# A hybrid HGRN2 and pooling block: whole fp32 operands built by accumulating transfers, and the first token tile taken ahead of the meta rows

## What is computed

```python
z = jnp.concatenate([meta, x], axis=1)                     # 16 + 1024 rows
h = rms_norm(z, norm_w[l])
p = (h @ w_in[l] + b_in[l]).astype(f32)                    # 1040 x 1024 by 1024 x 8192
q, fz, iv, g_hg, u, g_pool, m_hg, m_pool = jnp.split(p, split_at, axis=-1)
...
y_hg = (o * jax.nn.silu(g_hg)) @ w_down_hg[l]
y_pool = (mixed * pool_scale[l] * jax.nn.silu(g_pool)) @ w_down_pool[l]
merged = jax.nn.sigmoid(m_hg) * y_hg + jax.nn.sigmoid(m_pool) * y_pool
z = z + merged @ w_out[l]
...
return rms_norm(z, final_norm_w)[:, N_META:]
```

## Time and profile before

| what | value |
|---|---|
| median of 3 runs | 1035.59 us (1034.6 to 1035.83) |
| the profiled execution's own time | 1035.04 us |
| its span in the profile | 1033.3 us |
| PE busy | 1011.4 us, 98% of the span |
| DVE busy | 815.1 us, 79% |
| ACT busy | 512.2 us, 50% |
| POOL busy | 99.8 us, 10% |

### The profile page before, as it was taken

One profiled execution on the slowest core, in us unless ns is written; L12 is line 12 of the kernel. 1 busy time (PEld: TensorE's weight loads), 2 busy tenths in 40 slices (PEclk: granted clock), 3 DMA queues, 4 the chain that ended last, 5 costly groups with the idle time before them and its releaser, 6 DMA issues.

```text
span 1033.3 us, 18578 instructions
## 1 busy us (share of the span) xinstructions
PE 1011.4 (98%) x7204; PEld 827.7 (80%) x7204; DVE 815.1 (79%) x1343; ACT 512.2 (50%) x860; POOL 99.8 (10%) x162
## 2 busy tenths in 40 slices
PE   7999999999999999999999999999999999999996
PEld 7767888888878888878888888888887888788885
DVE  7989787868787878777676778876678879988975
ACT  7764636363636353544453534344447436435664
POOL 6200000101010101010101010102110010000130
PEclk9999999999999999999999999999999999999999
DMA  7221111202020202022213121227883384558374
GB/s 279 52 82 63 42 62 31 74 21 83 22 83 22 83 22 78 27 72 83 82 42 112 42 95 59 92 82 267 305 289 103 118 324 149 214 185 325 79 166 124
DMA packets 46855, 117.18 MB, mean 113 GB/s; under 512 B 4880, under 2 KB 13072, under 8 KB 46768
## 3 DMA queue, kind: packets, MB, share of 16 engines
q1 hardware_dynamic: 23680, 70.33, 20.5%
q0 software_dynamic: 8976, 26.26, 8.0%
q10 hardware_dynamic: 14112, 19.41, 5.5%
HBM read 86.62 MB, written 29.36 MB: 112 GB/s over the span
## 4 chain that ended last, share of the span: by engine, by line
PE 89%; DVE 8%; issue 2%; ACT 1%; DMA 1%; POOL 0%; DVEq 0%; SPq 0%; ACTq 0%
PE acc L1622 74%; PE levels L1677 2%; PE miscs L1711 1%; PE miscs L1710 1%; PE miscs L1699 1%; DVE r_lo L2489 1%; PE acc L1564 1%; PE miscs L1504 1%; PE levels L1504 1%; DVE w_lo L1900 1%; PE levels L1622 1%; PE levels L1683 1%; PE miscs L1717 1%; PE miscs L1690 1%; PE miscs L1652 1%
## 5 line engine op out<-in xcount | busy, mean ns | idle before, releaser
L1622 PE MATMUL acc<-r_hi,w_hi 128*128 128x512 f32 x1200 | 331.0, 397 | 3.5 <-ACT second L994 1.1
L1622 PE MATMUL acc<-r_lo,w_hi 128*128 128x512 f32 x1200 | 328.4, 392 | 0.5 <-DVE r_lo L2489 0.4
L1622 PE MATMUL acc<-r_hi,w_lo 128*128 128x512 f32 x1200 | 322.0, 390 | 0.5 <-DVE w_lo L1900 0.5
L1622 PEld LDWEIGHTS acc<-r_lo,w_hi 128*128 128x128 f32 x1200 | 223.0, 188 | 53.5 <-issue 4.9
L1622 PEld LDWEIGHTS acc<-r_hi,w_lo 128*128 128x128 f32 x1200 | 225.1, 188 | 49.1 <-DVE w_lo L1900 1.0
L1622 PEld LDWEIGHTS acc<-r_hi,w_hi 128*128 128x128 f32 x1200 | 218.6, 188 | 50.2 <-DVE zq L1994 2.3
L904 ACT ACTIVATE w_hi<-sum 128x512 fp32r<-128x512 f32 x164 | 102.9, 628 | 166.9 <-DVE sum L1933 84.7
L1900 DVE TENSOR_TENSOR w_lo<-sum,w_hi 128x512 fp32r<-128x512 f32 x164 | 112.0, 687 | 51.2 <-ACT w_hi L904 50.5
L1900 DVE TENSOR_TENSOR w_lo<-raws,w_hi 128x512 fp32r<-128x512 f32 x120 | 82.2, 687 | 48.6 <-ACT w_hi L904 48.6
L904 ACT ACTIVATE w_hi<-raws 128x512 fp32r<-128x512 f32 x120 | 74.6, 623 | 27.3 <-PE acc L1622 25.4
L994 ACT ACTIVATE second<-acc,bias 128x512 f32<-128x512 f32 x31 | 21.2, 685 | 59.9 <-PE acc L1622 59.8
(11 more groups left out here) (312 smaller groups left out, 1307.5 us busy)
## 6 DMA issues: line engine op xcount, KB each, us to landing
raws<-in_wstream SPq DMA_DIRECT2D x80, 512.0 KB, 3.6
xin<-in_x SPq DMA_DIRECT2D x8, 512.0 KB, 6.3
a_spill<-gt POOLq DMA_DIRECT2D x16, 256.0 KB, 3.5
c_spill<-pg POOLq DMA_DIRECT2D x16, 256.0 KB, 2.7
comb<-in_wstream ACTq DMA_DIRECT2D x8, 512.0 KB, 6.5
comb_spill<-comb ACTq DMA_DIRECT2D x8, 512.0 KB, 4.1
smh_spill<-zq POOLq DMA_DIRECT2D x16, 256.0 KB, 4.4
stage<-a_spill ACTq DMA_DIRECT2D x4, 1024.0 KB, 10.2
```

Source lines behind the costliest of these rows:

```text
L1622: ins = pe.matmul(bank[:, :], weights, moving, start=n == 0 and i in (0, 1, y_first), stop=n == 3 * KH - 1, skip_group_check=True)
```

## The change

- `nw` is loaded by SP instead of ACT. SP's order becomes x tile 1, nw, meta, tiles 2 to 4, raw weights 0 and 1, then tiles 5 to 7, raw 2, tile 8.
- Tile 1 goes through all engines ahead of the meta tile (`turn` swaps the two).
- Each of tiles 1, 2, 3, 4, 6, 8 gets banks of its own turn (`h_banks` is a table by tile).
- The fp32 B11 is no longer copied by DVE and the fp32 B21 no longer by ACT. SP copies the finished high part to a whole buffer within SBUF (`begin_whole`), and POOL issues a transfer that adds the low part to it (`make_whole`), 1 MB each, B11 first, B21 second.
- ACT writes -B12 into V7's slot and B22 into a buffer of its own, and POOL's `make_v7` adds B22 to -B12 by an accumulating transfer. `make_v4` does the same with V6 onto B21; the sign goes into ACT's scale and DVE's `v4_low`.
- The second half of the lb chain on DVE (four small operations) moves from ahead of tile 3 to behind `low(16)`.
- `early_sum`, `low(2)`, `low(4)` and `b21_low` change places on DVE; `meta_product(0)` moves between products (0,0) and (0,1); transposes 5 to 8 move later by one or two half products; `keep_warm` has 26 matmuls instead of 38.

```diff
-WARM_UP = (16, 4, 4, 4, 4)
+WARM_UP = ((1, 16), (0, 1), (2, 2), (3, 3), (4, 2))
...
         v6_whole = b11_whole = at("b11_whole", [P, KH, HALF], F32, R_AT + R_V4 * 16384)
+        b21_whole = at("b21_whole", [P, KH, HALF], F32, R_AT + R_V4 * 16384 + 8192)
+        b22_whole = at("b22_whole", [P, KH, HALF], F32, R_AT + R_V7 * 16384)
...
+            def begin_whole(n):
+                if n:
+                    sp.wait_ge(S["whole_begun"], 16)
+                    sp.wait_ge(S["h_copied"], 4)
+                    dst, src = b21_whole, r_hi[R_B21]
+                else:
+                    sp.wait_ge(S["h_hi"], 4)
+                    dst, src = b11_whole, r_hi[R_B11]
+                sp.dma_start(dst[:, :, :], src[:, :, :].bitcast(F32)).then_inc(S["whole_begun"], 16)
...
+            load_x(1)
+            sp.dma_start(nw[:, :], norm_w[0:1, :].to_broadcast([P, D])).then_inc(S["norm_row_loaded"], 16)
             sp.dma_start(xin[0][0:META, :], meta[:, :]).then_inc(x_loaded[0], 16)
-            load_x(1)
             load_x(2)
...
             begin_third(0)
+            begin_whole(0)
+            begin_whole(1)
             begin_third(1)
...
+            def make_whole(n):
+                pool.wait_ge(S["whole_begun"], 16 * n + 16)
+                if n:
+                    pool.wait_ge(S["whole_made"], 16)
+                    pool.wait_ge(S["h_lo"], 4)
+                    dst, src = b21_whole, r_lo[R_B21]
+                else:
+                    pool.wait_ge(S["b11_lo"], 4)
+                    dst, src = b11_whole, r_lo[R_B11]
+                pool.dma_start(dst[:, :, :], src[:, :, :].bitcast(F32), accum_op=ALU.add).then_inc(S["whole_made"], 16)
+
+            def make_v7():
+                pool.wait_ge(S["v5_made"], 4)
+                pool.wait_ge(S["h_copied"], CHUNKS)
+                pool.dma_start(r_lo_f[R_V7][:, :, :], b22_whole[:, :, :], accum_op=ALU.add).then_inc(S["v7_made"], 16)
+
+            def make_v4():
+                pool.wait_ge(S["v6_made"], 2)
+                pool.wait_ge(S["whole_made"], 32)
+                pool.dma_start(b21_whole[:, :, :], v6_whole[:, :, :], accum_op=ALU.add).then_inc(S["v4_made"], 16)
...
-                act.activation(b12_whole[:, :, c], lower, ACT.Copy)
-                act.activation(r_lo_f[R_V7][:, :, c], upper, ACT.Copy).then_inc(S["h_copied"], 1)
+                act.activation(r_lo_f[R_V7][:, :, c], lower, ACT.Copy, scale=-1.0)
+                act.activation(b22_whole[:, :, c], upper, ACT.Copy).then_inc(S["h_copied"], 1)
...
-            def b11_copy(i):
-                lower, _ = banks_of(i)
-                dve.tensor_copy(b11_whole[:, :, (i - 1) * P:i * P], lower)
...
             def v5_sum(i):
                 dve.wait_ge(S["h_copied"], i)
-                dve.tensor_tensor(r_lo_f[R_V6][:, :, piece(i)], b11_whole[:, :, piece(i)], b12_whole[:, :, piece(i)],
-                                  ALU.subtract).then_inc(S["v5_made"], 1)
+                dve.wait_ge(S["whole_made"], 16)
+                dve.tensor_tensor(r_lo_f[R_V6][:, :, piece(i)], b11_whole[:, :, piece(i)], r_lo_f[R_V7][:, :, piece(i)],
+                                  ALU.add).then_inc(S["v5_made"], 1)
```

More of the change, by code:

```diff
@@ L385, in hybrid_block @@
         VM, KM, KVM = slice(128, 256), slice(256, 384), slice(384, 512)
-        h_banks = ((misc[0], misc[1]), (lev, small))
+        h_banks = {i: (acc[2], acc[1]) if i == 3 else (acc[3], lev) if i == 4
+                   else (lev, small) if i in (1, 6, 8) else (misc[0], misc[1]) for i in range(CHUNKS + 1)}
         mix_banks = (lev, small, misc[0], misc[1])
@@ L1232, in _ @@
             high(9)
+            high(10)
             v7_high(0)
             v7_high(1)
-            high(10)
             copy_second(0)
@@ L1737, in mixing @@
                     ins.then_inc(S["mix_mm"], 1)
-            for i in range(5):
-                keep_warm(WARM_UP[i])
+            for i, n in WARM_UP:
+                keep_warm(n)
                 h_transposes(i)
-            keep_warm(6)
+            keep_warm(2)
             product(0, 0)
-            half(0, 1, 0)
+            meta_product(0)
+            product(0, 1)
             h_transposes(5)
-            half(0, 1, 1)
+            half(1, 0, 0)
             h_transposes(6)
-            half(1, 0, 0)
+            half(1, 0, 1)
             h_transposes(7)
-            half(1, 0, 1)
+            half(1, 1, 0)
             h_transposes(8)
-            for p, i in ORDER[3:2 * PRODUCTS]:
+            half(1, 1, 1)
+            for p, i in ORDER[4:2 * PRODUCTS]:
                 product(p, i)
@@ L2270, in _ @@
             v6_sum(0)
+            low(7)
             v6_sum(1)
-            low(7)
             v6_low(0)
```

238 lines of the change are left out of this document (119 added, 119 removed).

## The result

The changed kernel took 1036.82 us, the median of 20 runs (1034.03 to 1044.11), beside 1035.56 us of the kernel before in as many runs on the same chip: a ratio of 1.002, with a 95% interval of 1.0011 to 1.0029. Forecast was 1033.2. It is 1.3 us slower, not 2.4 us faster.

The account below looks back on a forecast made before the run. DVE was taken as the full engine in the first stage (37.34 to 69.46 us). A 5.0 us gain without later waits, cut by waits for V7 and V4, left -2.4: 1035.59 - 2.4 = 1033.2 us, range 1030.1 to 1040.2.

Parts of the forecast that it names:

- these stand in one POOL queue, and all are issued by 46.6: POOL's queue, first stage: B21's addition, second third sum, V7 and V4 follow in line; V7 there at 51.9, V4 at 57.2.
- the copy: SP's B11 copy waits for the last high part (19.0) and 1.3 MB ahead of it; landed at 25.0.
- the clock: PE's granted clock, 1.00 in every stretch, so the smaller `keep_warm` costs nothing as far as rows go.
- POOL's power of tile 7 stands behind this issue; the issue ends at 25.9, the power is wanted at 26.6: POOL's queue, front: tile 7's power follows the issue of B11's addition and still comes in time.
- (0,5): Product on PE needing tile 8's low part: starts at 36.45 instead of 37.34, PE waiting 1 us.
- DVE's relief: Four B11 copies (2.4 us) and four V7 and V4 half sums (4.6 us) leave DVE: 7 us lighter by the stage's end.
- X: DMA time of one 1 MB adding transfer: taken as 5.3 us, between 3.9 and 7.1.
- rivals A: First stage: transfers hidden, X up to 4.9, V4 at 55.6 or sooner, no wait, -5.0 us, 1030.6; chance 0.18.
- Rival C: First stage: additions cost by the byte, X = 7.1, V4 at 64.3, +4.6 us, 1040.2; chance 0.24.
- rival B: First stage: gain eaten, X 5.6 to 6.5, V4 at 58.4 to 62, 1034.4 to 1037.5; chance 0.15.
- ACT over 8 us behind V7: Sign in the changed profile: ACT waiting that long for V7's transfer would show Rival C; about 3.5 us was forecast.
- V4 = 36 + 4X: End of POOL's chain of additions: V4's landing time in us, 57.2 at the forecast X, wanted at 54.1.

Follow-up runs that it names:

- the upper group: Slower runs of the changed kernel, unaltered: three of the first 20, at 1042.7 to 1044.1 us; the profiled execution, 1043.8 us, is one of them.
- the lower group: Faster runs of the changed kernel, unaltered: seventeen of the first 20, at 1034.0 to 1038.5 us; its profile, taken on a later occasion, is of a 1034.38 us run.

## Why the prediction was wrong

**The step that failed in the profiled run and the upper group** is a clause on POOL's queue: "these stand in one POOL queue, and all are issued by 46.6". It priced the five masks between B21's addition and V7's at nothing. In the kernel before none had taken over 1.41 us; there they ran in the front, where DVE has waits and operations that read PSUM. Moved to 37.5 us they stand beside a DVE that works from two SBUF operands without a pause, and the first took 10.18 us. The additions went out at 51.43 and 51.96, V7 landed at 59.6 for the forecast 51.9. The prediction itself had counted against the change that POOL holds all six transfers in one line; it counted the transfers and not the masks between them.

**The steps that failed in the lower group, and so in the median,** are two others. In its profile the masks cost PE next to nothing: V7 is issued at 46.18, as forecast, and PE waits 0.86 us ahead of (0,4), hardly less than with the masks moved behind (0.99). There the copy and the clock are what was mis-sized.

*The copy.* It was forecast to land at 25.0. With SP's order as in the change, POOL could issue the addition behind it only at 25.88 to 28.23. "POOL's power of tile 7 stands behind this issue; the issue ends at 25.9, the power is wanted at 26.6" had 0.7 us to spare, and where it stood behind the issue the power came at 26.96 to 28.87. (0,5) started at 38.04 in the profile of the lower group, at 37.65 to 38.30 in versions that differ only behind it, and at 38.96 and 39.37 with the masks ahead, not at 36.45. Why the copy lands up to 2.3 us later in one profile than in another is not shown.

*The clock.* "Clock: 1.00 in every stretch" was read from a kernel whose longest wait in the stage was 1.1 us, and no sum had a price for a lower one, though the list of signs named it. In the lower group a wait of 2.87 ahead of (0,5) was followed by a clock of 0.79 over 36 to 44 us: the product took 4.42 us instead of 2.75. With the 1.6 us of the late start that is 3.3 us late at (1,5), and the stage ends at 69.72, not 67.1. In the upper group the clock stood at 0.52 for the three passes behind the wait of 7.80, 2.4 us.

**What held.** Product (0,0) (19.0 forecast, 19.06), tile 4's row (15.8, 15.87), (0,5) in the profiled run (36.45, 36.90), DVE's relief (7 us forecast; busy 815.1 us before and 808.1 now), and X (5.3, measured 5.1 to 5.4), against rivals A and C both. Tile 1 itself came 0.7 us sooner than forecast (square at 4.67 for 5.4), but that was gone by tile 2's row (11.61, forecast 11.4). With the hold and the copy out of the way (the copy sooner, masks ahead) the kernel took 1033.5 us, the forecast being 1033.2. But that agreement is partly luck: its profiled stage ended at 69.01, not 67.1, as B21's addition went out at 37.3 and not 35.9, V7's shared the engines with it until 48.4, and (0,4) started at 56.6 instead of 54.75.

**The rivals.** The time fell in rival B's span, 1034.4 to 1037.5, for none of B's reasons: X was not 5.6 to 6.5. Rival C's sign, "ACT over 8 us behind V7", appeared (10.96) with X as forecast; a sign that two causes can give does not tell them apart. No rival said that the queue's other work could be slow. Two of the rivals' sums are slightly off by the prediction's own terms: B's stage end of 71.9 gives 1038.0, not 1037.5, and at X = 6.0, V4 = 36 + 4X puts the stage's end at 69.9, not 69.5. Neither bears on the result.

**Still open.** What starts a long hold: why the masks in the kernel before, placed at 47.7 us beside equally dense DVE work, were held for 2.2 us only, and whether the addition issued just ahead has a part in it. That the small writes open a way for POOL rests on one profile and on the upper group's absence or shift in two kernels. And what decides whether PE's clock falls behind a wait of 2.4 to 2.6 us: the same wait did both, in kernels that are alike there.

## What to carry to other kernels

Work that moves to another queue is not only its own cost: list what stands between two of its issues, and read each of those at its new time, not at its old one. A GpSimd operation with an SBUF source that stands ahead of something awaited belongs where VectorE has gaps or reads PSUM; here moving five small masks was worth 7 us between two medians of one occasion. When a median hides two groups, get a profile of each: the two groups here had different causes, and the copy's help alone, which moved (0,5) ahead as meant, left 6 of 7 runs in the upper group. And before two single profiles are subtracted, compare their clocks over the whole span: here 1.5 us came and went 390 us behind the change.
